# A three-layer forward pass on one core: small products of the RWKV mixers in bursts, and work moved from VectorE to GpSimd and ScalarE

## What is computed

```python
def rwkv7_step(state, inp):
    r, decay, k, v, kk, a = inp
    sa = jnp.einsum('bhij,bhj->bhi', state, -kk)
    state = (state * decay[:, :, None, :]
             + sa[..., None] * (kk * a)[:, :, None, :]
             + v[..., None] * k[:, :, None, :])
    out = jnp.einsum('bhij,bhj->bhi', state, r)
    return state, out
...
    y = ((y - mu) * lax.rsqrt(var + LNX_EPS)).reshape(b, s, D_RWKV) * lnx_g.astype(f32) + lnx_b.astype(f32)
    bonus = jnp.sum(r * k * r_k.astype(f32), axis=-1, keepdims=True) * v
    y = (y + bonus.reshape(b, s, D_RWKV)) * g
```

## Time and profile before

| | us |
|---|---|
| median of 3 runs | 3603.29 (3601.32 to 3614.74) |
| the profiled execution's own time | 3605.12 |
| its span | 3603.3 |
| TensorE busy | 3413.4 (95%) |
| VectorE busy | 1670.0 (46%) |
| ScalarE busy | 1171.4 (33%) |
| GpSimd busy | 486.6 (14%) |

### The profile page before, as it was taken

How to read it: one execution, slowest core, us unless ns; L and a number is a source line. 1 busy time by engine, 2 the same in 40 slices (tenths; PEclk the granted TensorE clock), 3 DMA queues, 4 the chain that set the end, 5 groups by cost and what they waited for, 6 DMA issues and landing times.

```text
span 3603.3 us, 54151 instructions
## 1 busy us (share of the span) xinstructions
PE 3413.4 (95%) x22733; PEld 1935.2 (54%) x22733; DVE 1670.0 (46%) x2661; ACT 1171.4 (33%) x2083; POOL 486.6 (14%) x477
## 2 busy tenths in 40 slices
PE   8999999999799999989999999988999999899999
PEld 4455555655233333445565656555555666466654
DVE  2555666644311118334454455453226555455541
...
GB/s 115 24 65 70 49 42 61 89 48 117 298 345 392 308 344 398 88 18 1 18 18 18 18 18 6 8 132 18 78 0 12 1 1 14 24 1 1 1 27 67
DMA packets 115385, 302.58 MB, mean 84 GB/s; under 512 B 13143, under 2 KB 55447, under 8 KB 101959
## 3 DMA queue, kind: packets, MB, share of 16 engines
...
...
## 4 chain that ended last, share of the span: by engine, by line
PE 85%; DVE 7%; ACT 3%; DMA 2%; issue 2%; POOL 1%; SPq 1%; DVEq 0%; ACTq 0%; POOLq 0%
PE ps L2796 11%; PE ps L448 9%; PE ps L2242 8%; PE ps L2271 8%; PE ps L3508 7%; PE ps L1812 6%; PE ps L2814 5%; PE ps L3780 3%; PE ps L3189 3%; PE ps L1248 3%; PE ps L1832 3%; PE ps L3461 2%; PE ps L2480 2%; DMA sb<-in_exp_up 1%; PE ps L3169 1%
## 5 line engine op out<-in xcount | busy, mean ns | idle before, releaser
L2796 PE MATMUL ps<-sb 128*128 128x512 f32 x960 | 461.1, 599 | 19.6 <-ACT sb L2154 10.9
L2242 PEld LDWEIGHTS ps<-sb 128*128 128x128 f32 x2624 | 287.9, 141 | 302.5 <-ACT sb L2250 129.9
L2242 PE MATMUL ps<-sb 128*128 128x128 f32 x2624 | 417.2, 282 | 19.4 <-DVE sb L2258 9.5
L2250 ACT ACTIVATE sb<-ps 128x512 f32<-128x512 f32 x336 | 200.2, 597 | 714.6 <-PE ps L2242 714.6
L2216 ACT ACTIVATE sb<-ps,sb 128x1280 f32<-128x1280 f32 (+1 forms) x288 | 353.4, 1232 | 130.4 <-DVE sb L2209 111.9
L2258 DVE COPY sb<-ps 128x512 f32<-128x512 f32 x320 | 220.0, 689 | 372.6 <-PE ps L2242 371.9
L448 PE MATMUL ps<-sb 128*128 128x512 f32 x704 | 349.1, 615 | 8.7 <-ACT sb L654 4.1
L3508 PE MATMUL ps<-sb 96*128 96x512 f32 (+1 forms) x768 | 331.8, 525 | 8.7 <-DVE sb L3565 7.2
L2271 PEld LDWEIGHTS ps<-sb 128*64 128x64 f32 x5248 | 284.2, 137 | 70.4 <-issue 40.2
L2271 PE MATMUL ps<-sb 128*64 128x128 f32 x5248 | 318.5, 275 | 3.3 <-DVE sb L2258 3.1
L2037 POOL TENSOR_TENSOR sb<-sb 128x1 f32<-128x1 f32 (+3 forms) x114 | 132.1, 1160 | 1054.0 <-DVE sb L2033 1054.0
...
## 6 DMA issues: line engine op xcount, KB each, us to landing
...
```

Source lines behind the costliest of these rows:

```text
L2242: ins = k.pe.e.transpose(k.bank(bank)[:, 128 * j:128 * j + 128], self.Pb[g % 2][:, 1280 * b + 128 * c:1280 * b + 128 * c + 128], k.f(C_ID, ...
L2250: k.act.e.activation(self.PT[:, xs[0]:xs[-1] + 1, :], k.bank(bank)[:, 0:128 * len(xs)].rearrange("p (j t) -> p j t", j=len(xs)), ACT.Copy) ...
L2796: ins = pe.e.matmul(k.bank(5), lhs[:, kk, :], w[:, kk, 512 * half:512 * half + 512], start=kk == 0, stop=kk == 7)
```

## The change

Eight edits, all inside `mixers`:

1. The product for the inverse leaves "ab" and becomes a step "zb" of its own, twice per pair: 16 products of 64x64 weights (32 rows in the trace's counting) for four chunks at once, of 128 and of 64 columns by turns, over the whole of banks 6 and 7. `fill` orders ab 0, zb 0, ab 1, ab 2, turn, ab 3, turn, zb 1, ab 4, turn, ab 5, turn, ab 6, ab 7.
2. ScalarE takes each zb out in two activations of 128x512, where it had 16 small ones for four chunks.
3. Of the six takings-out of transposes per pair ScalarE does five (it did three), VectorE one.
4. Half 1 of zr goes to GpSimd (two 128x512 multiplications). "rk" and the end of the preparation now also wait for it. The minus sign moves from zr into ctr_kn, and a second one into scaled_b.
5. VectorE's part of v's shift becomes a step "shift_v", behind the third burst of the inversions; the transposes of v (tail_turn 4 and 5) go from behind burst 1 to behind burst 3.
6. Variance, logarithm, exponential and norm of the closing each go one gap later; the outputs stay.
7. `steps` for f < 5: two projection matmuls instead of one behind burst 1, one instead of two behind bursts 4 and 9, three instead of two behind burst 11. So the sixteenth matmul of k stays behind burst 9, and the first of r goes from there to behind burst 11.
8. "ctr" goes from step 8 to 9 of 24 and "ctr_ex" from 10 to 11.

```diff
     def fill(f):
-        return weave([("ab", c) for c in range(8)], [("tail_turn", f, n) for n in range(4)])
+        return ([("ab", 0), ("zb", 0), ("ab", 1)] + weave([("ab", 2), ("ab", 3)], [("tail_turn", f, 0), ("tail_turn", f, 1)])
+                + [("zb", 1)] + weave([("ab", c) for c in range(4, 8)], [("tail_turn", f, 2), ("tail_turn", f, 3)]))
 
...
-        closing = {0: ["fin_mean"], 1: ["fin_sq"], 3: ["fin_var"], 4: ["fin_ln"], 5: ["fin_exp"]}
+        closing = {0: ["fin_mean"], 1: ["fin_sq"], 4: ["fin_var"], 5: ["fin_ln"], 6: ["fin_exp"]}
...
             for half in range(2):
-                side[6 + half].append(("fin_norm", f - 1, half))
+                side[7 + half].append(("fin_norm", f - 1, half))
+            for half in range(2):
                 side[8 + half].append(("fin_out", f - 1, half))
             side[9].append(("fin_store", f - 1))
-        side[1] += [("tail_turn", f, 4), ("tail_turn", f, 5)]
+        side[2].append(("shift_v",))
+        side[3] += [("tail_turn", f, 4), ("tail_turn", f, 5)]
         side[5].append(("rk", f))
...
-        steps = (0, 1, 2, 1, 2, 2, 2, 2, 3, 2, 0, 2, 1, 1, 3) if f < 5 else (0, 0, 0, 0, 1, 2, 2, 1, 1, 1, 0, 2, 2, 0, 0)
+        steps = (0, 2, 2, 1, 1, 2, 2, 2, 3, 1, 0, 3, 1, 1, 3) if f < 5 else (0, 0, 0, 0, 1, 2, 2, 1, 1, 1, 0, 2, 2, 0, 0)
...
-        at_step = {1: ("kk_sum", f, 0), 3: ("kk_sum", f, 1), 4: ("kk_rsqrt", f), 6: ("ctr_scale", f), 8: ("ctr", f), 10: ("ctr_ex", f), 13: ("ctr_kn", f),
+        at_step = {1: ("kk_sum", f, 0), 3: ("kk_sum", f, 1), 4: ("kk_rsqrt", f), 6: ("ctr_scale", f), 9: ("ctr", f), 11: ("ctr_ex", f), 13: ("ctr_kn", f),
...
+        elif kind == "zb":
+            half, = x
+            pe.wait_ge(*t["zr", half])
+            pe.wait_ge(*t["bT"])
+            pe.wait_ge(*free[6])
+            pe.wait_ge(*free[7])
+            for c in range(4 * half, 4 * half + 4):
+                for r in range(2):
+                    for h in range(2):
+                        of_t = slice(128 * (c % 4), 128 * (c % 4) + (64 if r else 128))
+                        ins = pe.e.matmul(k.bank(6 + h)[halves[r ^ h], of_t], bT[halves[h], 128 * c + 64 * r:128 * c + 64 * r + 64],
+                                          zr[halves[h], c, 0, 64 * r:128], start=True, stop=True, skip_group_check=True)
+            ins.then_inc(*product.up())
...
             pe.wait_ge(*t["bT"])
-            for h in range(2):
-                pe.wait_ge(*free[6 + h])
-                ins = pe.e.matmul(k.bank(6 + h)[:, 0:128], bT[halves[h], cs], zr[halves[h], c, 0, :], start=True, stop=True)
-            ins.then_inc(*product.up())
-            t["zbmm"] = product.at
...
-            if n % 2:
+            if n != 4:
                 dst = (Bt, Kt, Vt)[n // 2]
                 b = 4 + n % 2
                 act.wait_ge(*t["tailturn"])
                 act.wait_ge(*t["scan_end"])
-                act.e.activation(dst[:, 4:8, :], k.bank(b).rearrange("p (j t) -> p j t", j=4), ACT.Copy).then_inc(*evac_a.up())
+                act.e.activation(dst[:, 4 * (n % 2):4 * (n % 2) + 4, :], k.bank(b).rearrange("p (j t) -> p j t", j=4), ACT.Copy).then_inc(*evac_a.up())
                 free[b] = t["tok1"] = evac_a.at
...
-        elif kind == "ab":
-            c, = x
-            v = k.ps[:, 3072:4096].rearrange("p (h t) -> p h t", h=2)
-            up, low = halves
+        elif kind == "zb":
+            half, = x
             act.wait_ge(*t["zbmm"])
-            j = 2 * (c % 4)
-            act.e.activation(zb[c // 4][up, j, :], v[up, 0, 0:128], ACT.Copy)
-            act.e.activation(zb[c // 4][low, j, 0:64], v[low, 0, 64:128], ACT.Copy).then_inc(*evac_a.up())
-            free[6] = evac_a.at
-            act.e.activation(zb[c // 4][low, j + 1, :], v[up, 1, 0:128], ACT.Copy)
-            act.e.activation(zb[c // 4][up, j + 1, 0:64], v[low, 1, 64:128], ACT.Copy).then_inc(*evac_a.up())
-            free[7] = t["zb", c // 4] = evac_a.at
+            for h in range(2):
+                act.e.activation(zb[half].rearrange("p (c h) t -> p h c t", h=2)[:, h], k.bank(6 + h).rearrange("p (c t) -> p c t", c=4), ACT.Copy).then_inc(*evac_a.up())
+                free[6 + h] = t["zb", half] = evac_a.at
...
             if name == "vT":
-                t["vT"] = shifted.at
+                t["v_scale"] = pc[:, m:m + 1]
+            else:
+                dve.e.scalar_tensor_tensor(out=dst, in0=raw[:, 0:1024], scalar=pc[:, m:m + 1], in1=dst, op0=ALU.mult, op1=ALU.add).then_inc(*shifted.up())
+                t["raw"] = t["shift", name] = shifted.at
+        elif kind == "shift_v":
+            dve.wait_ge(*t["unshifted"])
+            dve.e.scalar_tensor_tensor(out=vT, in0=raw[:, 0:1024], scalar=t["v_scale"], in1=vT, op0=ALU.mult, op1=ALU.add).then_inc(*shifted.up())
+            t["raw"] = t["vT"] = shifted.at
...
-            dve.e.scalar_tensor_tensor(out=T[2], in0=T[3], scalar=2.0 ** 10, in1=T[2], op0=ALU.mult, op1=ALU.mult).then_inc(*dve_out.up())
+            dve.e.scalar_tensor_tensor(out=T[2], in0=T[3], scalar=-2.0 ** 10, in1=T[2], op0=ALU.mult, op1=ALU.mult).then_inc(*dve_out.up())
...
-            dve.e.tensor_tensor(bT, bT, T[4], ALU.mult).then_inc(*dve_out.up())
+            dve.e.scalar_tensor_tensor(out=bT, in0=bT, scalar=-1.0, in1=T[4], op0=ALU.mult, op1=ALU.mult).then_inc(*dve_out.up())
...
-            dve.wait_ge(*t["ym", half])
-            dve.e.scalar_tensor_tensor(out=zr[:, cs, 0, :], in0=c8(T[2])[:, cs, :], scalar=-1.0, in1=c8(T[0])[:, cs, :], op0=ALU.mult, op1=ALU.mult)
+            dve.wait_ge(*t["ym", 0])
+            dve.e.tensor_tensor(zr[:, cs, 0, :], c8(T[2])[:, cs, :], c8(T[0])[:, cs, :], ALU.mult)
...
+            dve.wait_ge(*t["zr", 1])
...
-            t["prep_end"] = [t["tailturn"], t["tok0"], t["tok1"], t["bT0"], t["bv"]]
+            t["prep_end"] = [t["tailturn"], t["tok0"], t["tok1"], t["bT0"], t["bv"], t["zr", 1]]
...
+        elif kind == "zr" and x[1] == 1:
+            cs = slice(4, 8)
+            pool.wait_ge(*t["ex"])
+            pool.wait_ge(*t["kn"])
+            pool.wait_ge(*t["ym", 1])
+            pool.e.tensor_tensor(zr[:, cs, 0, :], c8(T[2])[:, cs, :], c8(T[0])[:, cs, :], ALU.mult)
+            pool.wait_ge(*t["ep"])
+            pool.wait_ge(*t["shift", "rm"])
+            pool.e.tensor_tensor(zr[:, cs, 1, :], c8(rm)[:, cs, :], c8(T[3])[:, cs, :], ALU.mult).then_inc(*pool_out.up())
+            t["zr", 1] = pool_out.at
...
```

19 lines of the change are left out of this document (8 added, 11 removed).

## The result

| | before | changed |
|---|---|---|
| median of the runs timed side by side | 3613.81 us (10 runs, 3601.32 to 3617.06) | 3591.75 us (10 runs, 3585.85 to 3596.57) |
| profiled execution, its span | 3605.12, 3603.3 us | 3590.77, 3588.9 us |
| granted clock, mean | 0.985 | 0.983 |

The ratio is 0.9944, 95% interval 0.9933 to 0.9955: some 20 us faster (22 between the medians), where 28 were forecast. A second measurement gave 0.9936 (0.9917 to 0.9954). The time, 3591.75 us, lies above the range (3560 to 3589). Part of that is the yardstick: the three runs of before that the forecast was set against had a median of 3603.29, ten of them 3613.81. On that yardstick the measured ratio would give 3583, inside the range; so the place of the time outside it is owed to the yardstick more than to the sum.

A forecast was written before the change was run, and what follows sets the result against it. TensorE was taken as the bound, busy 3413.4 of 3603.3 us. Pair 0's 8.3, pairs 1 to 4's 18.8 and pair 5's 0.9 make 28 us off 3605.1: 3577.1, as a median 3575; range 3560 to 3589.

The forecast's parts named there:

- What bounds the kernel; the mixers' gain passed on undiminished: Whole kernel: TensorE is busy 3413.4 of 3603.3 us; what the mixers save reaches the end in full.
- Without the shift VectorE goes on when bT is done: Ahead of pair 0's fill: VectorE resumes at 132.1 us, so the fill starts 3.0 us earlier (1.8 to 4.3).
- I take 3.6 us off: Pair 0's fill, 14.9 us at a granted clock of 0.83, gets 3.6 us shorter, most of the clock's loss staying.
- Fill, pairs 1 to 5, 2.8 us: From fill to first merge: the merge starts at 257.6 instead of 260.4 us, 2.8 us saved a pair.
- The rule on changes of tiling: Fill: tiling changes drain TensorE; four more at 0.37 to 0.39 us would give back 1.1 us a fill, forecast 3582.
- v's transposes, 0.9: Inversions: moving them behind burst 3 removes TensorE's wait, 0.9 us in pairs 1 to 4, 0.7 in pair 0.
- ctr, 1.0: Before scan_s: ctr one step later removes TensorE's idle time, 1.0 us in each of pairs 0 to 4.
- k's step, 0: Inversions: moving k's last step removes a 0.82 us wait, but VectorE's chain is late next; 0 (0 to 0.8).
- Last pair, +0.9: Pair 5: 2.8 us gained in its fill less 1.9 us of new waits, 0.9 us net.
- (b): Inversions: VectorE becomes the bound, its v shift coinciding with GpSimd's masks; 3595 us; 0.17 together with (c) and mixtures.
- (c): Fill: issue of small products, not waits for banks, sets it; 3591 us; 0.17 together with (b) and mixtures.
- (d): Fill: GpSimd's half of zr holds up zb 1, making the kernel slower; 3622 us and up; chance 0.02.

The follow-up runs named there:

- The combined kernel: Changed kernel with VectorE's wait behind v's case, zr wholly on VectorE, another fill order, k's last step and pair 5's gaps as before; 3578.27 us, ratio 0.9911.

## Why the prediction was off

- **What bounds the kernel; the mixers' gain passed on undiminished.** Right by the medians: 19.1 us at the last scan, 19.5 at the first fetch, 20.2 by the ratio (0.56% of 3613.81). The combined kernel's 15.7 were not passed on whole, so it is no rule.
- **"Without the shift VectorE goes on when bT is done".** This step failed, and cost most. Pair 0 was to give 8.3 us: 3.0 ahead of the fill, 3.6 in it, 0.7 and 1.0 behind it. It gave 1.2 + 0.8 + 0.3 + 1.0 = 3.3. The wait for v's evacuation stayed where it was, ahead of `if name == "vT"`; the rows of the order show operations and no waits, the code shows them. With the wait moved it is 2.7 + 1.9 + 0.3 + 1.0 = 5.9, the 2.7 within the bounds of 1.8 to 4.3 that I gave for GpSimd's part. With GpSimd's half of zr taken back too it is 4.6 + 3.6 + 0.3 + 1.0 = 9.5. So "I take 3.6 us off" for the fill held only where the clock did not fall at all. The fill's part is chance by up to 1.4 us: with the changed kernel's code and idle time ahead of it, it was 0.7, 0.8, 2.1 and 2.1 in four profiles. The wait's own share is the lead, 1.2 instead of 3.0.
- **Fill, pairs 1 to 5, 2.8 us.** It was 1.97, and the term was mis-sized, 4.1 us over five pairs. From the first burst's start to the merge 9.8 us were forecast, 10.5 measured. The bursts took 1.02 instead of 0.9 each (0.24 together): I compared with merge_b because of the alternating quarters and did not count the columns per quarter. The "ab" steps and their changes took 5.7 where 5.3 stood: 0.76 holds for an "ab" with a change of tiling on one side, and three of the seven have one on both, 0.86. The lead-in and the merge's wait make the remaining 0.2. The wait for ab 6's mask came as forecast, 0.50 us.
- **The rule on changes of tiling.** A change costs 0.1 us here (0.86 with two, 0.76 with one), not the 0.37 to 0.39 of a product that I priced the rule at. The bursts also add three changes per fill, not four (thirteen where ten stood). The Trainium skill (TensorEngine Tiling (Array Packing), Key Properties) says that TensorE drains at such a change; the rows show a gap, of that size.
- **v's transposes, 0.9; ctr, 1.0; k's step, 0.** Right as sizes (0.93, 1.02, -0.15 a pair). But the transposes' wait would have gone with the bursts alone, so 0.9 belongs to edits 1 to 3 as much as to edit 5. What edits 4 and 5 are needed for is the fill: without them VectorE's first masks stop TensorE 1.36 us.
- **Last pair, +0.9.** It was -0.6: 1.98 gained in the fill and 2.56 lost. I had 1.9 for new waits; without the clock they came to 1.4, of which 1.0 hangs on which engine went first. The fall to 1.2 GHz behind them, 1.15, was not in the sum, and the fill's 2.8 was too much here as well.
- **Rivals.** (b)'s mechanism, v's shift and GpSimd's masks excluding each other, is real but cost TensorE nothing in pairs 1 to 4; it counts in the last pair and at most 0.5 us in pair 0. (c) is refuted, ScalarE did set the fill; that its 3591 is the time measured is luck. (d) did not occur.

The sum by measured terms: 3.3 and the 0.8 ahead of pair 0, 4 x 3.9, less 0.6, are 19.1, where the forecast had 28. Of the difference, pair 0 is 5.0 (up to 1.4 of it the execution's), the fills of pairs 1 to 4 are 3.3, the last pair 1.5; the 0.8 goes the other way. Set against the ten runs' median of 3613.81, a gain of 28 would have meant 3586; the other 11 us of the forecast's error come from a median over three runs that lay low.
